# Another order for the products of a latent attention whose small norms stood alone

## What is computed

```python
ckv = rms_norm(h, kv_in_norm_g) @ w_dkv            # 256 latent + 64 rotated key columns
c, k_rope = ckv[..., :256], ckv[..., 256:]
c = rms_norm(c, kv_norm_g)                         # the small norm "kv"
kv = (c @ w_ukv).reshape(B, S, 8, 256)             # keys ukv_k and values ukv_v
k_rope = apply_rope(k_rope)
cq = rms_norm(rms_norm(h, attn_norm_g) @ w_dq, q_norm_g)   # the small norm "q", 384 wide
q = (cq @ w_uq).reshape(B, S, 8, 192)              # uq_n: 8 x 128, uq_r: 8 x 64, rotated
p = softmax(mask((q_nope @ k_nope + q_rope @ k_rope) * scale))
h = h + (p @ v) @ w_o_b
```

## Time and profile before

| what | value |
|---|---|
| median of three runs | 3245.77 us (3244.35 to 3249.53) |
| the profiled execution, its time | 3253.55 us |
| its span, first to last instruction | 3251.8 us |
| PE busy (matmuls) | 2748.6 us, 85% |
| DVE, ACT, POOL busy | 61%, 44%, 51% |
| the core's mean granted TensorE clock | 0.924 |
| latent attention before the scores, half 0 | 1991.6 to 2089.1 us |
| the same, half 1 | 2888.6 to 2970.0 us |

### The profile page before, as it was taken

The page is one execution under the profiler, slowest core; times in us unless marked ns, Lnnn a source line. Parts: engine busy times, 40 slices in busy tenths (PEclk is TensorE's granted clock), DMA queues, the critical chain, the costliest instruction groups (busy, mean ns, idle before and its releaser), DMA issues. The chain is left out here.

```text
span 3251.8 us, 42976 instructions
## 1 busy us (share of the span) xinstructions
PE 2748.6 (85%) x15302; PEld 2108.8 (65%) x15302; DVE 1976.1 (61%) x4160; ACT 1436.4 (44%) x3190; POOL 1666.8 (51%) x1014
## 2 busy tenths in 40 slices
PE   6987997796778787769889997779997999988898
PEld 3855996573333332228558786547876978987898
DVE  5675444347776776767677667767666364254423
ACT  2222222222343333345776555676554454443543
POOL 4712221254444443337437885537874607852675
PEclk8988998898999899989789998899997999998999
DMA  7210001226999999888979998979995405542454
GB/s 282 104 65 1 1 1 52 91 78 257 421 421 421 421 421 421 342 338 327 366 271 360 396 408 352 369 274 366 411 406 226 143 14 175 177 130 71 130 176 124
DMA packets 140517, 797.46 MB, mean 245 GB/s; under 512 B 15505, under 2 KB 18705, under 8 KB 67601
## 3 DMA queue, kind: packets, MB, share of 16 engines
q0 software_dynamic: 73728, 536.90, 40.6%
q1 hardware_dynamic: 65856, 253.36, 22.3%
q10 hardware_dynamic: 720, 4.46, 0.3%
HBM read 788.10 MB, written 6.55 MB: 244 GB/s over the span
## 5 line engine op out<-in xcount | busy, mean ns | idle before, releaser
L299 POOL TENSOR_TENSOR wls<-raws,whs 128x1024 fp32r<-128x1024 f32 (+1 forms) x256 | 610.5, 2394 | 380.0 <-ACT whs L293 372.6
L1739 PE MATMUL ps<-raw,un 128*128 128x512 f32 x714 | 369.0, 634 | 86.5 <-ACT un L1800 85.7
L1720 POOL DMA_INDIRECT raw<-in_peer_uv,un x253 | 258.5, 1022 | 263.9 <-PE ps L1739 174.3
L1793 ACT ACTIVATE un<-un 128x1 f32<-128x1 f32 x512 | 103.6, 202 | 626.4 <-DVE scratch L1842 615.1
L1941 PE MATMUL ps<-ts,whs 128*128 128x256 f32 x1424 | 302.9, 313 | 28.7 <-DVE ts L2031 19.2
L299 POOL TENSOR_TENSOR wlw<-raws,whw 128x1024 fp32r<-128x1024 f32 x112 | 267.6, 2403 | 89.0 <-ACT whw L293 88.2
L293 ACT CAST whs<-raws 128x1024 fp32r<-128x1024 f32 (+1 forms) x256 | 263.9, 1036 | 94.3 <-PE ps L2493 34.5
L1941 PEld LDWEIGHTS ps<-ts,whs 128*128 128x128 f32 x1424 | 242.5, 206 | 61.4 <-issue 42.8
L1739 PEld LDWEIGHTS ps<-raw,un 128*128 128x128 f32 x714 | 127.8, 199 | 231.2 <-ACT un L1800 151.2
L1739 PE MATMUL ps<-w,un 128*128 128x512 f32 x384 | 201.9, 669 | 89.1 <-ACT un L1800 89.1
L2493 PE MATMUL ps<-ts,whs 128*128 128x256 f32 x1216 | 239.8, 298 | 0.0
(11 more groups left out here) (435 smaller groups left out, 7133.1 us busy)
## 6 DMA issues: line engine op xcount, KB each, us to landing
raws<-in_w_up SPq DMA_DIRECT2D x128, 512.0 KB
raws<-in_w_down SPq DMA_DIRECT2D x128, 512.0 KB
raws<-in_w_qk SPq DMA_DIRECT2D x32, 512.0 KB
scratch<-in_ada_w SPq DMA_DIRECT2D x13, 1024.0 KB, 14.4
raw<-in_w_in SPq DMA_DIRECT2D x11, 1024.0 KB, 5.6
raw<-in_ada_w SPq DMA_DIRECT2D x11, 1024.0 KB, 4.8
raw<-in_peer_w_q SPq DMA_DIRECT2D x8, 1024.0 KB, 6.9
raws<-in_w_v SPq DMA_DIRECT2D x16, 512.0 KB
```

What stands on the lines that cost most here:

```text
L299: e.tensor_tensor(self.wl[h][:, 0:width], self.raw[slot][:, 0:width], self.wh[h][:, 0:width].bitcast(F32), ALU.subtract).then_inc(*self.ti ...
L1720: e.indirect_dma_start(self.rows[r], None, self.d["peer_uv"], index).then_inc(*self.tick(f"row{r}", n, 16))
L1739: ins = e.matmul(self.ps[:, b + half, :], self.diag[n % 4], self.rows[self.row_of(n)][:, 1024 + 512 * half:1536 + 512 * half], start=k == ...
L1793: e.activation(self.gelus[:, c], self.dots[:, c], ACT.Gelu, bias=0.0, scale=1.0).then_inc(*self.tick(S))
```

## The change: what it does

- The order of the weight tiles, and of the products, becomes w_dkv, w_dq, ukv_k, ukv_v, uq_r, uq_n. w_dq reads its input from H.A, which "next" fills at the end of the MLP before and beside w_dkv.
- The rotation of the key part and the sums of the norm kv stand on PE behind the first tile of w_dq; the roots, the scaling and the high and low parts of kv stand beside the other two tiles. The scaled tiles of w_dq go to a buffer of their own, ccq.
- The sums of the norm q stand on PE behind the last tile of ukv_k; its root, scaling, high and low parts beside ukv_v, into H.A[2..4].
- uq_r comes ahead of uq_n, and the rotations of the queries' tiles 0, 1 stand behind the second tile of uq_n, those of 2, 3 behind its fourth.
- The four turns of the two norms go: 15.5 turns up to the scores, where there were 19.5.
- The two loads of the rotation tables stand on SP's queue before w_dq's second tile, which is the fifth tile as ukv_k's second was. Each score waits for the queries' tile of its head, where the first waited for all.

```diff
-    for part in (..., 0, ("w_dkv", "ukv_k", "ukv_v", "w_dq", "uq_n", "uq_r", "w_o_b"), 1):
+    for part in (..., 0, ("w_dkv", "w_dq", "ukv_k", "ukv_v", "uq_r", "uq_n", "w_o_b"), 1):
...
+            H.ccq = [plain(f"ccq{h}{i}", t + 3072 + 256 * i, 256) for i in range(3)]
...
 def pe_mla
-        def norm(tile, last_y):
+        def sums(tile, last_y):
             e.wait_ge(*self.at(D_, (tile, "sq")))
             self.tail_spread_sums(e, H.gel[0], (S, tile, "sums"), S, (tile, "sums"), (D_, (tile, "y", last_y)))
-            yield 1
-            yield 1
+        def beside_dq(j):
+            if j == 0:
+                self.pe_rope(e, S, "k", H.kpe, (D_, ("w_dkv", 2)), D_)
+                sums("kv", 1)
+        def beside_uq(j):
+            for i in (j - 1, j) if j in (1, 3) else ():
+                self.pe_rope(e, S, i, H.qr[:, i, :], (A_, ("qr", i)), D_)
         yield from self.tail_gemm(e, H, "w_dkv", ...)
-        self.pe_rope(e, S, "k", H.kpe, (D_, ("w_dkv", 2)), D_)
-        yield from norm("kv", 1)
+        yield from self.tail_gemm(e, H, "w_dq", lambda k: H.A[k], lambda k: (D_, ("next", k)), ..., beside_dq)
         yield from self.tail_gemm(e, H, "ukv_k", ...,
+                                  lambda j: sums("q", 2) if j == 7 else None)
         yield from self.pe_values(e, H, "ukv_v", ...)
-        yield from self.tail_gemm(e, H, "w_dq", lambda k: H.B[k], ...)
-        yield from norm("q", 2)
-        yield from self.tail_gemm(e, H, "uq_n", lambda k: H.A[k], ...)
-        yield from self.tail_gemm(e, H, "uq_r", lambda k: H.A[k], ...)
-        for j in range(4):
-            self.pe_rope(e, S, j, H.qr[:, j, :], (A_, ("qr", j)), D_)
+        yield from self.tail_gemm(e, H, "uq_r", lambda k: H.A[2 + k], lambda k: (D_, ("q", "ul", k)), ...)
+        yield from self.tail_gemm(e, H, "uq_n", lambda k: H.A[2 + k], None, ..., beside_uq)
         yield 1
...
 def dve_mla
         for c in range(3):                       # beside w_dkv
+            if c == 0: following(0..3)           # lows of next
             if c == 1: reciprocal of the root
             scale the tiles of w_dkv             # 0 and 1 at c == 1, 2 at c == 2
+            if c == 1: following(4..7)
             yield 1
+        for c in range(3):                       # beside w_dq
+            if c == 0: add("kv", 2)
+            if c == 1: scaled("kv"); dve_rope("k")
+            scale the tiles of w_dq              # 0 and 1 at c == 1, 2 at c == 2
+            if c == 2: lows("kv", 2, 0)
+            yield 1
         for j in range(8):                       # beside ukv_k
+            if j == 0: add("q", 3)
             if j % 2 == 0: copy kn
         for c in range(2):                       # beside ukv_v
+            if c == 1: scaled("q"); lows("q", 3, 2)
             copy vm
+            if c == 0: memset kr, two copies into kr
             yield 1
+        for j in range(4): yield 0.375           # beside uq_r
         for j in range(8):                       # beside uq_n
             if j % 2 == 0: copy qn
+            for i in (j - 1, j) if j in (1, 3) else (): dve_rope(i)
             yield 0.375
...
 def act_mla: following(0..3) before w_dkv, following(4..7) behind the root at its first tile;
+  beside w_dq: squares and root of kv at c == 0, highs at c == 2; beside ukv_k: squares of q;
+  beside ukv_v: root of q at c == 0, highs at c == 1; then the copies of uq_r, then of uq_n
...
 def sp_tail
-            if key[0] == "ukv_k" and key[1] == 1:
+            if key[0] == "w_dq" and key[1] == 1:
```

More of the change, by code:

```diff
@@ L168, in tail_keys @@
     order = []
-    for part in (("w_qk", "w_v", "w_o_a"), 0, ("w_dkv", "ukv_k", "ukv_v", "w_dq", "uq_n", "uq_r", "w_o_b"), 1):
+    for part in (("w_qk", "w_v", "w_o_a"), 0, ("w_dkv", "w_dq", "ukv_k", "ukv_v", "uq_r", "uq_n", "w_o_b"), 1):
         order += mlp(part) if isinstance(part, int) else [(name, c) for name in part for c in range(TILES[name][1])]
@@ L2645, in act_mla, with following, squares, highs @@
         S, D_, P_ = f"mla{h}_act", f"mla{h}_dve", f"mla{h}_pe"
-        def norm(tile, n, dim):
-            for i in range(n):
-                e.wait_ge(*self.at(D_, ("w_dkv" if tile == "kv" else "w_dq", 2)))
-                e.activation(H.gel[1 + i % 2] if i else H.gel[0], H.cc[:, i, :], ACT.Square, bias=0.0,
+        g2 = self.gain("attn_norm_g_2", 8)
+        def following(j):
+            e.activation(H.A[j][0], self.xT[:, j, H.hs], ACT.Identity, bias=0.0,
+                         scale=g2(j)).then_inc(*self.tick(S, ("next", j)))
+        def squares(tile, cc):
+            for i in range(len(cc)):
+                e.activation(H.gel[1 + i % 2] if i else H.gel[0], cc[i], ACT.Square, bias=0.0,
                              scale=1.0).then_inc(*self.tick(S, (tile, "sq", i)))
-            self.act_root(e, (P_, tile, "sums"), P_, (tile, "sums"), S, (tile, "root"), dim, 0)
-            yield 1
+        def highs(tile, n, first):
             for i in range(n):
                 e.wait_ge(*self.at(D_, (tile, "y", i)))
-                e.copy(H.A[i][0], H.gel[i]).then_inc(*self.tick(S, (tile, "uh", i)))
-            yield 1
+                e.copy(H.A[first + i][0], H.gel[i]).then_inc(*self.tick(S, (tile, "uh", i)))
+        e.wait_ge(*self.at(f"mlp0{h}_pe", ("v", 7, 7)))
+        for j in range(4):
+            following(j)
         for c in range(3):
@@ L2664, in act_mla @@
                 self.act_root(e, (P_, "sums"), P_, "sums", S, "root", D, 0, H.gel[3])
+                for j in range(4, 8):
+                    following(j)
             self.act_ahead(e, "w_dkv", c, h)
             yield 1
-        yield from norm("kv", 2, 256)
-        g2 = self.gain("attn_norm_g_2", 8)
+        for c in range(3):
+            if c == 0:
+                e.wait_ge(*self.at(D_, ("w_dkv", 2)))
+                squares("kv", [H.cc[:, i, :] for i in range(2)])
+                self.act_root(e, (P_, "kv", "sums"), P_, ("kv", "sums"), S, ("kv", "root"), 256, 0)
+            e.wait_ge(*self.at(P_, ("w_dq", c)))
+            if c == 2:
+                highs("kv", 2, 0)
+            self.act_ahead(e, "w_dq", c, h)
+            yield 1
         for j in range(8):
-            e.activation(H.B[j][0], self.xT[:, j, H.hs], ACT.Identity, bias=0.0,
-                         scale=g2(j)).then_inc(*self.tick(S, ("next", j)))
-        for j in range(8):
+            if j == 0:
+                e.wait_ge(*self.at(D_, ("w_dq", 2)))
+                e.wait_ge(*self.at(D_, ("kv", "ul", 1)))
+                squares("q", H.ccq)
             e.wait_ge(*self.at(P_, ("ukv_k", j)))
@@ L2683, in act_mla @@
             yield 1
-        for c in range(3):
-            e.wait_ge(*self.at(P_, ("w_dq", c)))
-            self.act_ahead(e, "w_dq", c, h)
-            yield 1
-        yield from norm("q", 3, 384)
+        for j in range(4):
+            e.wait_ge(*self.at(P_, ("uq_r", j)))
+            e.copy(H.qr[:, j, :], self.bh((P_, "uq_r", j))).then_inc(*self.tick(S, ("qr", j)))
+            if j % 2:
+                self.act_ahead(e, "uq_r", j // 2, h)
+            yield 0.375
         for j in range(8):
@@ L2732, in dve_mla, with following, add @@
         S, A_, P_ = f"mla{h}_dve", f"mla{h}_act", f"mla{h}_pe"
-        def norm(tile, n, gain):
+        g2 = self.gain("attn_norm_g_2", 8)
+        def following(j):
+            hi, lo = H.A[j]
+            e.wait_ge(*self.at(A_, ("next", j)))
+            e.scalar_tensor_tensor(out=lo, in0=self.xT[:, j, H.hs], scalar=g2(j), in1=hi.bitcast(F32), op0=ALU.mult,
+                                   op1=ALU.subtract).then_inc(*self.tick(S, ("next", j)))
+        def add(tile, n):
             for i in range(1, n):
@@ L2738, in norm, with scaled @@
                 e.tensor_tensor(H.gel[0], H.gel[0], H.gel[1 + i % 2], ALU.add).then_inc(*self.tick(S, (tile, "sq") if i == n - 1 else None))
-            yield 1
+        def scaled(tile, cc, gain):
             r = self.bh((P_, tile, "sums"))
```

95 lines of the change are left out of this document (52 added, 43 removed).

## The result

The changed kernel takes 3225.23 us (median of four runs, 3224.18 to 3231.28) against 3247.65 us for the kernel before on the same chip: a ratio of 0.9935, 95% interval 0.9918 to 0.9953. It is 0.65% faster, an interval clear of 1, and by about the forecast. Measured again with the experiments it took 3218.47 us (six runs, 3212.50 to 3225.81) against 3247.26, a ratio of 0.9914 (0.9897 to 0.9932).

What follows compares the result with a forecast made beforehand. TensorE bounds it, idle in three stretches per latent attention. Half 1's 15.9 us plus half 0's 5 give 21 off 3253.6 us profiled, 3232.6; the runs' median lies 7.8 lower, so 3225 us, range 3204 to 3242.

Steps and rivals of the forecast that it cites:

- Half 1, 15.9 us forecast: Half 1's latent attention stage: 13.8 us gained from TensorE's stalls plus 2.1 from low clock; bounds 9 to 27.
- w_dq's first tile's end and the sums: Half 1, norm kv's input and sums: TensorE would stall 2.8 us, where there were 8.1.
- the first score: Half 1, queries' rotations partly covered by uq_n: TensorE would wait 4.8 us before the scores, where there were 7.2.
- That just fits: Half 1, norm kv's root, reciprocal, scalings and rotation fit beside 5.76 us of w_dq; 1.1 us of wait left behind.
- The sum for uq_r: Half 1, norm q: 7.1 us of chain beside 5.5 us of ukv_v, stall 1.4 us where there were 8.6.
- The low clock of half 1, 2.1 us gained: Slow matmuls after gaps cost 6.6 us; 2.5 at the scores and 2.0 behind the first stall stay.
- Half 0's stalls, 6 gained, 14 left: Half 0's stage, four PSUM banks: of 20.1 us of waits 14 stay, 6 gained; bounds none to 45.
- The turns, 3.8 gained and 4.5 lost: Half 0: 4.4 expert rows leave the stage, gaining 3.8 us, and go to the second MLP's end, losing 4.5.
- The whole cover: Rival: VectorE slips into GpSimd's gaps and banks come in time; 27 us in half 1, 15 in half 0; 3204 us, 17%.
- The port's rival: Rival: at half 1's rotations all eight two-SBUF-input VectorE operations each wait a whole GpSimd low; 3235 us, 11%.
- Four banks give half 0 nothing: Rival: half 0's bank waits equal the old 20 us; it ends 1 us up, half 1 keeps 15; 3231 us, 17%.
- The slower outcome: Rival: VectorE's queue in half 0 makes bank waits total 45 us where 20 went; 3255 us, 6%.

Runs made afterwards that it cites:

- first profile: Profile taken with the changed kernel's first measurement, unaltered, against the kernel before: median 3225.23 us, ratio 0.9935.
- second profile: Profile of the same changed kernel, unaltered, measured once more beside the follow-up experiments: median 3218.47 us, ratio 0.9914.
- the experiments on the turns: Changed kernel with its four removed turns put back: at the stage's end 3234.73 us, or in pairs behind w_dq and ukv_v 3225.41 us.
- five edits more: Changed kernel plus late w_o_b roundings, early w_dq remainders, queries' root in SBUF, earlier queries' norm, latent's tiles elsewhere in half 1: 3204.82 us, ratio 0.9868.

## Why the prediction was right, step by step

The total (3225.0 forecast, 3225.23 and 3218.47 measured) is right, and so are most parts of half 1; in half 0 two errors have opposite signs. That the first profile's span came out 22.3 us shorter, where 21 were forecast, is in part luck: by the same cut the two stages and half 0's attention and second MLP give 14.8 us of it, and 22.5 of the second profile's 28.3; the rest stands in the other stretches. Which order of rotation and remainder the executions without a profile had is not known.

*Half 1, 15.9 us forecast.* The stage lost 13.4 us in the first profile and 17.5 in the second. The waits in us:

| wait before | forecast | first profile | second |
|---|---|---|---|
| w_dq's first tile's end and the sums | 2.8 | 2.41 | 2.27 |
| ukv_k | 1.1 | 4.54 | 1.18 |
| uq_r | 1.4 | 1.28 | 1.28 |
| the first score | 4.8 | 4.68 | 4.68 |

The count of queued instructions gave three of four to within 0.6 us. The fourth, "That just fits", is so only if GpSimd's remainder comes after the rotation. The working put remainders of POOL beside the "next" and beside the queries' rotations, but none beside the norm kv's own rotation, though ScalarE rounds a weight tile after each of w_dq's tiles. That is the step that failed, in two profiles of ten; the reciprocal's and the scalings' lengths were right (1.77 and 0.87 us, for 1.77 and 1.0). The sum for uq_r, 7.1 us beside 5.5, makes 1.6 and not 1.4, which changes nothing.

*The low clock of half 1, 2.1 us gained:* from the second profile 17.5 of stage less 14.5 of waits leaves 3.0, and from the first 13.4 less 11.0 leaves 2.4. TensorE's busy time for the stage's 336 matmuls says the same: 55.6 us before, 52.7 and 52.6 after. Right.

*Not undone.* What the queries' norm and the rotations gave in half 1 is shown by edits that undo them. The latent's norm, 8.1 us of waiting before and 3.5 in the second profile (w_dq and ukv_k), has no such edit; its gain is read from the waits.

*Half 0's stalls, 6 gained, 14 left.* The waits seen behind w_dkv sum to 13.0 us, but at other places in part: none before w_dq's third tile (4 forecast), 2.94 before the latent's sums (none forecast), 5.81 before ukv_v's second pair (5), 2.67 before uq_n's fifth tile (2.5), none before the first score (2.5). The stage lost 7.2 us and the turns account for 4.3, so the stalls gave 2.9, not 6. One reason is where the sum started. Its 20.1 us are the three stretches less their rows and norms at full speed, but TensorE was without work there for only 4.1 + 4.8 + 6.4 = 15.3 us; the rest was slow matmuls, and the 14 that were to stay were counted as waits alone. The prediction kept no slow clock in half 0; the stage's granted clock is 0.87 after and 0.88 before, and with the norm ahead of the turn it is 0.92 and TensorE's busy time some 4 us less (66.59 for 70.74). What the waits gave, slow matmuls behind the 5.81 us in part took (a granted clock of 0.69 in the 6 us behind it).

*The turns, 3.8 gained and 4.5 lost.* The gain is 4.3 by the experiment. The loss was mis-sized: the sum took 1.1 us for each of the four turns, and four more rows in the second MLP cost 0 to 2 us, as the experiments on the turns show. Attention and second MLP of half 0 together were 387.7 us before and 393.6 and 389.9 after. That is mostly scatter: in the ten profiles with the change's number of rows there the two take 389.8 to 393.7 us, 391.7 on average, and in the three with four rows fewer 387.7, 391.6 and 394.4. (The last row stood some 13 us before the second MLP's end, not the 4.1 us of the working, which means some four turns and goes on with 11.5 us.) The two errors of half 0 nearly cancel: 5 forecast, 1.4 and 5.0 found from the first MLP's end to the second's. That this part came out so near is luck.

*The rivals.* The whole cover (3204 us) did not come with the change, but its picture of half 1 was right about what is there to get: with five edits more the stage lost 28.2 us against the kernel before, for 27, and the total reached 3204.82. In half 0 the stage lost 11.8, where 15 was the picture for the half. The port's rival was wrong in number, four instructions and not eight, and right in kind. "Four banks give half 0 nothing" was right for the queries' norm, whose cover is worth nothing in half 0; for the whole it was too low, since the stalls gave 2.9 us, midway between its nothing and the 6 of the forecast. The Trainium skill, Perfetto Trace Analysis, "Optimization Strategy", which reads recurring gaps as missing buffers or PSUM, fits 3.3 of the 5.81 us, by the run with the root in SBUF; the rest was the chain. The slower outcome did not come near: it decided from 36 us of stalls on, and 13 stand in half 0, the largest 5.8.

## What to carry to other kernels

Covering a norm's chain with the next product is worth the chain only where the queue that runs it is free: count what stands ahead of it on each engine, and what another engine holds of it. Look for work of GpSimd that nobody needs soon (here the remainders of w_o_b) beside short VectorE instructions that TensorE waits for, and move it into a stretch where TensorE is the bound: that one move of four roundings took 6.5 us off half 1's stage, more than any single part of the change that was undone (5.4 for the cover of the queries' norm, 2.4 for the rotations). An operand moved from PSUM to SBUF can undo such a gain, as the root did. And where a sum ends in "just fits", read more than one profile: one may show the wait and another not.

## What was not expected of the hardware

Two instructions on two engines, started 0.05 us apart, decided 3.4 us of TensorE's waiting in an unchanged program. A slower clock went with the shorter stage: in the second profile the matmuls behind the latent's sums had a granted clock of 0.70 against 0.89, the rounding that starts the remainder stood behind them, 5.22 us after the sums instead of 4.13, and so the rotation came first; the stage's mean clock was 0.88 against 0.90, and its length 62.2 us against 66.3. The ten profiles with this order of instructions fit one line. In five the clock in the 5.2 us behind the sums is 0.67 to 0.70, the rounding comes 5.08 to 5.22 us after them, and the rotation is ahead by 0.75 us or more; in four it is 0.85 to 0.89, the rounding comes after 4.13 to 4.31 us, and the two start within 0.14 us of each other, in either order. The last, with w_dq's remainders early, waits for nothing inside w_dq's first tile: its clock is 1.00, its rounding comes after 3.58 us, and the remainder is ahead by 0.13 us. So the long wait there was likely no accident of that profile but what its faster matmuls brought. That the clock came first and the order after it is read from these ten profiles; no experiment set the clock.
